# Spread products of a wide and a narrow expert block: one set for two blocks, summed in PSUM

## The reference

```python
gu = xb @ w_gate_up[e] + b_gate_up[e]                 # xb: a block of tokens of expert e
glu = jnp.minimum(gu[:, :D_FF], SWIGLU_LIMIT)
lin = jnp.clip(gu[:, D_FF:], -SWIGLU_LIMIT, SWIGLU_LIMIT)
act = glu * jax.nn.sigmoid(SWIGLU_ALPHA * glu) * (lin + 1.0)
yb = (act @ w_down[e] + b_down[e]) * g[:, None]       # g: the gate of each token
out = jnp.zeros((n_tok, d), n.dtype).at[slot_tok].add(yb.reshape(rows, d))
```

## Time and profile before

| | us |
|---|---|
| median of 3 runs | 1469.05 (1467.71 to 1469.11) |
| the profiled execution | 1468.26 |
| its span in the trace | 1466.7 |
| TensorE busy | 1449.4 (99%) |
| VectorE busy | 784.3 (53%) |
| ScalarE busy | 381.3 (26%) |
| GpSimd busy | 223.8 (15%) |

### The profile page before, as it was taken

One profiled execution on the slowest core, in us unless ns is written; L12 is line 12 of the kernel. 1 busy time (PEld: TensorE's weight loads), 2 busy tenths in 40 slices (PEclk: granted clock), 3 DMA queues, 4 the chain that ended last, 5 costly groups with the idle time before them and its releaser, 6 DMA issues.

```text
span 1466.7 us, 35402 instructions
## 1 busy us (share of the span) xinstructions
PE 1449.4 (99%) x13987; PEld 810.7 (55%) x13987; DVE 784.3 (53%) x1560; ACT 381.3 (26%) x669; POOL 223.8 (15%) x448
## 2 busy tenths in 40 slices
PE   8999999999999999999999999999999999999997
PEld 6998989977874344344443444434444344443444
DVE  6767999968646435444354443544435444354444
ACT  3634323345332012211122111221112111121114
POOL 1000000000014322121121211212112121121000
PEclk9999999999999999999999999999999999999998
DMA  3322333141339899999999999999999999999991
GB/s 135 111 69 105 116 116 114 72 177 66 116 115 346 340 383 419 401 424 419 420 424 423 424 421 415 424 423 425 418 419 425 418 423 420 417 424 418 427 417 64
DMA packets 45840, 459.46 MB, mean 313 GB/s; under 512 B 10177, under 2 KB 10690, under 8 KB 15458
## 3 DMA queue, kind: packets, MB, share of 16 engines
q1 hardware_dynamic: 37538, 450.74, 74.6%
q0 software_dynamic: 8256, 8.08, 1.7%
HBM read 456.37 MB, written 4.43 MB: 314 GB/s over the span
## 4 chain that ended last, share of the span: by engine, by line
PE 92%; DVE 4%; DMA 3%; ACT 1%; issue 0%; SPq 0%; DVEq 0%; ACTq 0%
PE bank L1937 55%; PE bank L1618 16%; PE bank L1999 10%; PE bank L1809 6%; DMA n_scratch<-reg_b 1%; DMA ring<-in_moe 1%; DVE w_lo L1035 1%; PE bank L1746 1%; PE bank L1749 1%; PE bank L1761 0%; PE bank L1747 0%; PE bank L1776 0%; DVE reg_tq L1125 0%; DVE reg_tq L1051 0%; PE bank L1637 0%
## 5 line engine op out<-in xcount | busy, mean ns | idle before, releaser
L1937 PE MATMUL bank<-ring,moe_f 128*32 128x256 f32 (+1 forms) x10296 | 835.5, 485 | 0.6 <-DVE moe_f L1530 0.4
L1937 PEld LDWEIGHTS bank<-ring,moe_f 128*32 128x32 f32 x10296 | 331.3, 110 | 500.6 <-issue 393.5
L943 ACT ACTIVATE moe_f<-moe_f 128x768 f32<-128x768 f32 (+1 forms) x32 | 23.8, 745 | 748.8 <-DVE moe_f L1517 748.8
L1552 DVE TENSOR_TENSOR reg_a<-reg_a,bank 128x512 f32<-128x512 f32 x240 | 146.7, 682 | 126.1 <-PE bank L1999 126.0
L1511 DVE STREAM_TRANSPOSE moe_f<-bank 128x768 f32<-128x768 f32 (+1 forms) x32 | 27.5, 859 | 321.6 <-PE bank L1937 315.6
L1618 PE MATMUL bank<-n_hi,w_hi 128*128 128x258 f32 (+2 forms) x608 | 190.6, 313 | 1.8 <-DVE w_lo L1035 1.8
L1618 PE MATMUL bank<-n_lo,w_hi 128*128 128x258 f32 (+2 forms) x608 | 186.4, 306 | 0.0
L1618 PE MATMUL bank<-n_hi,w_lo 128*128 128x258 f32 (+2 forms) x608 | 186.2, 306 | 0.0
L659 POOL DMA_INDIRECT moe_f<-n_scratch,idx_next x75 | 81.6, 1088 | 427.2 <-DVE moe_f L1492 410.1
L1999 PE MATMUL bank<-reg_b_r,reg_x_r 96*128 96x512 f32 (+1 forms) x504 | 144.3, 431 | 0.3 <-DVE reg_x_r L1539 0.3
L952 ACT COPY moe_f<-bank 32x256 f32<-32x256 f32 x324 | 118.0, 364 | 23.3 <-PE bank L1937 19.6
(11 more groups left out here) (301 smaller groups left out, 1181.6 us busy)
## 6 DMA issues: line engine op xcount, KB each, us to landing
ring<-in_moe SPq DMA_DIRECT2D x184, 2048.0 KB, 14.7
ring<-in_w_in SPq DMA_DIRECT2D x24, 1024.0 KB, 4.9
ring<-in_moe SPq DMA_DIRECT2D x13, 1024.0 KB, 11.7
ring<-in_w_out SPq DMA_DIRECT2D x8, 1024.0 KB, 4.8
ring<-acs_scratch SPq DMA_DIRECT2D x4, 1024.0 KB, 6.8
reg_vcs<-in_xT SPq DMA_DIRECT2D x4, 528.0 KB, 6.0
reg_x<-in_xrow SPq DMA_DIRECT2D x4, 512.0 KB, 5.2
n_scratch<-reg_b SPq DMA_DIRECT2D x4, 512.0 KB, 2.9
```

Source lines behind the costliest of these rows:

```text
L1552: v.tensor_tensor(h2[:, u // 2, c], h2[:, u // 2, c], bank[:, 5 + u % 3, :], ALU.add).then_inc(added, 1)
L1937: ins = mm(out[l * LANE:(l + 1) * LANE, g * width:(g + 1) * width], x[:, at, g * LANE:(g + 1) * LANE], w[:, l * width:(l + 1) * width], st ...
```

## The change

Blocks are added two at a time. A set now holds the wide block 2n and the narrow block 2n+1 (for n = 0 blocks 0 and 1, both wide): each unit is four products, high and low of the one and of the other, summed in the same bank, then one addition. The sets stand in the loops of the narrow blocks alone, where the eight units come in two fours with two G between them; the loops of the wide blocks, and that of block 2, have none. The wide blocks' rows are at home in `reg_b`, the narrow ones' in `reg_tq` over 64 rows; both homes get a copy of the bias rows for the first set. DVE's `add_rows` runs once for a pair, at the head of its loop body. TensorE's loops for blocks 3 and 4 are written out ahead of the loop over p.

```diff
-TURNS = "GGGGDDAAAAAAAAGGDDGGDDDD"
+TURNS = "GGGGDDGGDDGGDDDD"
+TURNS_ADDING = "GGGGDDAAAAGGAAAADDGGDDDD"
...
-        split_in, split_last = reg_b_r[:, 0:2 * D], reg_tq_r[:, 0:2 * D]
+        split_rows_of = [reg_b_r[:, 0:2 * D], reg_tq_r[:, 0:2 * D]]
+        all_w, all_n, bias_rows = slice(0, BLOCK), slice(0, NARROW * LANE), slice(BLOCK, P)
+        wide_home, narrow_home, second_home = (0, all_w), (1, all_n), (1, all_w)
...
-            def high(j, to=split_in):
-
+            def high(j, home):
+
+                n, rows = home
                 act.wait_ge(y_ready, j + 2)
-                if j is not FIRST and to is split_in:
-                    act.wait_ge(acc_done, j * UNITS)
-                a.activation(to[0:BLOCK, 0:D], y_tok[0:BLOCK, :], ACT.Copy, scale=cols[0:BLOCK, ds(j + LIST, 1)]
+                a.activation(split_rows_of[n][rows, 0:D], y_tok[rows, :], ACT.Copy, scale=cols[rows, ds(j + LIST, 1)]
                              ).then_inc(y_hi_tok, 1)
...
-            a.copy(split_in[BLOCK:P, 0:D], y_tok[BLOCK:P, :]).then_inc(gm_high, 1)
+            for n in range(2):
+                a.copy(split_rows_of[n][bias_rows, 0:D], y_tok[bias_rows, :]).then_inc(gm_high, 1)
...
             with act.Fori(0, n_pairs - 1) as p:
                 sigmoid(2 * p + 3, NARROW)
                 evict(2 * p + 2, WIDE)
-                high(2 * p + 2)
+                act.wait_ge(acc_done, p * UNITS + UNITS)
+                high(2 * p + 2, wide_home)
...
-            def add_rows(j):
+            def add_rows(n):
 
                 for u in range(UNITS):
                     c = slice(u % 2 * 512, (u % 2 + 1) * 512)
-                    dve.wait_ge(acc_done, j * UNITS + (u + 1))
+                    dve.wait_ge(acc_done, n * UNITS + (u + 1))
                     v.tensor_tensor(h2[:, u // 2, c], h2[:, u // 2, c], bank[:, 5 + u % 3, :], ALU.add).then_inc(added, 1)
...
-            dve.wait_ge(idx_moved, 1)
-            v.tensor_scalar(spread[1][0:BLOCK, :], tok_iota[0:BLOCK, :], 0.0, None, ALU.mult).then_inc(gm_low, 1)
-            dve.wait_ge(gm_high, 2)
+            dve.wait_ge(gm_high, 3)
...
-            v.tensor_tensor(split_in[BLOCK:P, D:2 * D], y_tok[BLOCK:P, :], split_in[BLOCK:P, 0:D].bitcast(F32), ALU.subtract
-                            ).then_inc(gm_low, 1)
-            split_rows(FIRST, 0, 2 * IDX_W)
-            add_rows(FIRST)
+            for n in range(2):
+                to = split_rows_of[n]
+                v.tensor_tensor(to[bias_rows, D:2 * D], y_tok[bias_rows, :], to[bias_rows, 0:D].bitcast(F32), ALU.subtract
+                                ).then_inc(gm_low, 1)
+            split_rows(FIRST, wide_home, 2 * IDX_W)
...
             with dve.Fori(0, n_pairs - 1) as p:
+                add_rows(p)
                 activations(2 * p + 3, expert_of(2 * p + 3), NARROW, (p * (16 * (WIDE + NARROW)) + 16 * (2 * WIDE + NARROW), WIDE))
-                split_rows(2 * p + 2, 0, p * (IDX_W + IDX_N) + 3 * IDX_W)
-                add_rows(2 * p + 2)
+                split_rows(2 * p + 2, wide_home, p * (IDX_W + IDX_N) + 3 * IDX_W)
                 activations(2 * p + 4, expert_of(2 * p + 4), WIDE, (p * (16 * (WIDE + NARROW)) + 32 * (WIDE + NARROW), NARROW))
-                split_rows(2 * p + 3, 1, p * (IDX_W + IDX_N) + (3 * IDX_W + IDX_N))
-                add_rows(2 * p + 3)
+                split_rows(2 * p + 3, narrow_home, p * (IDX_W + IDX_N) + (3 * IDX_W + IDX_N))
+            add_rows(n_pairs - 1)
...
+            def spread_of(home, rows, u, out, opens, closes):
+
+                to, hf = slice(u // 2 * P, (u // 2 + 1) * P), u % 2 * 512
+                split = split_rows_of[home]
+                mm(out, spread[home][rows, to], split[rows, hf:hf + 512], start=opens, stop=False)
+                return mm(out, spread[home][rows, to], split[rows, D + hf:D + hf + 512], start=False, stop=closes)
+
+            def adding_unit(n, u):
+
+                first = n is FIRST
                 if u == 0:
+                    rows_split(2 * n + 2)
+                    if not first:
+                        pe.wait_ge(added, n * UNITS)
                 if u >= 3:
+                    pe.wait_ge(added, n * UNITS + (u - 2))
+                out = bank[:, 5 + u % 3, :]
+                spread_of(0, slice(0, P) if first else all_w, u, out, True, False)
+                spread_of(1, slice(0, P) if first else all_n, u, out, False, True).then_inc(acc_done, 1)
...
-            woven(THIRD, WIDE, WIDE, 0)
+            woven(THIRD, WIDE, WIDE)
...
-            with pe.Fori(0, n_pairs - 1) as p:
-                woven(2 * p + 3, NARROW, WIDE, 1)
-                woven(2 * p + 4, WIDE, NARROW, 0)
-            woven(n_blocks - 1, NARROW, WIDE, 1)
+            pe.wait_ge(gm_high, 3)
+            pe.wait_ge(gm_low, 3)
+            woven(3, NARROW, WIDE, FIRST)
+            woven(4, WIDE, NARROW)
+            with pe.Fori(1, n_pairs - 1) as p:
+                woven(2 * p + 3, NARROW, WIDE, p)
+                woven(2 * p + 4, WIDE, NARROW)
+            woven(n_blocks - 1, NARROW, WIDE, n_pairs - 1)
```

More of the change, by code:

```diff
@@ L986, in _ @@
                 act.wait_ge(idx_moved, p * (IDX_W + IDX_N) + (3 * IDX_W + IDX_N))
-                high(2 * p + 3)
+                high(2 * p + 3, narrow_home)
             sigmoid(n_blocks - 1, NARROW)
             evict(n_blocks - 2, WIDE)
-            high(n_blocks - 2)
+            act.wait_ge(acc_done, n_pairs * UNITS)
+            high(n_blocks - 2, wide_home)
             a.activation(small[:, 7:8], ones[:, 0:1], ACT.Sqrt).then_inc(rs_root, 1)
@@ L1530, in activations, with split_rows @@
                 v.tensor_tensor(act_last if last else act_rows(n), up, sig, ALU.mult).then_inc(act_ready, 1)
-            def split_rows(j, n, columns, to=split_in):
+            def split_rows(j, home, columns):
+                n, rows = home
+                to = split_rows_of[n]
                 dve.wait_ge(idx_moved, columns)
[L1535 to L1539, removed]
+                v.tensor_scalar(spread[n][rows, :], tok_iota[rows, :], cols[rows, ds(j, 1)], None, ALU.is_equal
                                 ).then_inc(spread_ready, 1)
                 dve.wait_ge(y_hi_tok, j + 1)
[L1542 to L1545, removed]
-            def add_rows(j):
+                v.scalar_tensor_tensor(to[rows, D:2 * D], y_tok[rows, :], cols[rows, ds(j + LIST, 1)],
+                                       to[rows, 0:D].bitcast(F32), ALU.mult, ALU.subtract).then_inc(y_lo_tok, 1)
+            def add_rows(n):
                 for u in range(UNITS):
                     c = slice(u % 2 * 512, (u % 2 + 1) * 512)
-                    dve.wait_ge(acc_done, j * UNITS + (u + 1))
+                    dve.wait_ge(acc_done, n * UNITS + (u + 1))
                     v.tensor_tensor(h2[:, u // 2, c], h2[:, u // 2, c], bank[:, 5 + u % 3, :], ALU.add).then_inc(added, 1)
@@ L1561, in _ @@
             activations(SECOND, 1, WIDE, (16 * WIDE, WIDE), at=5)
-            dve.wait_ge(idx_moved, 1)
-            v.tensor_scalar(spread[1][0:BLOCK, :], tok_iota[0:BLOCK, :], 0.0, None, ALU.mult).then_inc(gm_low, 1)
-            dve.wait_ge(gm_high, 2)
-            v.tensor_tensor(spread[1][BLOCK:P, :], gm_rows[BLOCK:P, :], spread[0][BLOCK:P, :].bitcast(F32), ALU.subtract
+            dve.wait_ge(gm_high, 3)
+            v.tensor_tensor(spread[1][bias_rows, :], gm_rows[bias_rows, :], spread[0][bias_rows, :].bitcast(F32), ALU.subtract
@@ L1584, in _ @@
-            split_rows(n_blocks - 1, 1, n_pairs * (IDX_W + IDX_N) + 2 * IDX_W, split_last)
+            split_rows(n_blocks - 2, wide_home, n_pairs * (IDX_W + IDX_N) + (2 * IDX_W - IDX_N))
+            split_rows(n_blocks - 1, narrow_home, n_pairs * (IDX_W + IDX_N) + 2 * IDX_W)
             roots[0] += 1
@@ L1992, in rows_split @@
                 pe.wait_ge(y_lo_tok, n_blocks)
[L1994 to L2001, removed]
@@ L2003, in spread_unit @@
-            def spread_unit(j, u, s, out):
-                if u == 0:
[L2006 to L2011, removed]
-                if u >= 3:
-                    pe.wait_ge(added, j * UNITS + (u - 2))
-                if j is FIRST:
-                    spread_part(1, u, slice(0, P), split_in, out, True, False, (0,))
-                    return spread_part(s, u, slice(0, P), split_in, out, False)
-                return spread_part(s, u, slice(0, BLOCK), split_in, out)
@@ L2021, in woven @@
+            def woven(j, n, n_before, adds=None):
                 q = b = u = 0
-                for kind in TURNS:
+                for kind in TURNS if adds is None else TURNS_ADDING:
                     if kind == "G":
@@ L2029, in woven @@
                     else:
-                        spread_unit(FIRST if j is THIRD else j - 2, u, s, bank[:, 5 + u % 3, :]).then_inc(acc_done, 1)
+                        adding_unit(adds, u)
                         u += 1
@@ L2069, in last_bank @@
                 return bank[:, PART_BANKS[u // 2] + u % 2, :]
-            def first_part(u):
```

(5 more changed lines are left out.)

18 lines of the change are left out of this document (8 added, 10 removed).

## The result

The change makes the kernel slower: 1486.84 us (1485.62 to 1488.38, 4 runs) against 1469.08 (1467.71 to 1469.72, 4 runs), a ratio of 1.0123 with a 95% interval of 1.011 to 1.0136. The span of the profiled execution grew from 1466.7 to 1485.3 us.

The account below looks back on a forecast made before the run. Transfers were to bound the pairs at 61.0 us; 9.1 us earlier at the last wait (slack 3.4 + holes 5.7) against 3.0 for the double set gave -6.1: 1463.0 us, range 1459.2 to 1467.0.

Parts of the forecast that it names:

- Spacing of the products: In the adding sets: 0.236 us a product, so 32 products take 7.6 us; TensorE's work falls 1.5 us a pair.
- Rival (d): In the sets: something else paces them at 9.1 us, the pair stays 61.0, time within 2 us of now; chance 0.03.
- The transfers as the bound: In the pairs: DMA stays at 421 GB/s, 61.0 us a pair; TensorE waits about 1.5 us for the first down pair.
- Rival (a): In the pairs: transfers follow TensorE, the rate rising from 421 to 432 GB/s or more, time 1445; chance 0.04.
- Won back: Ahead of the third gate-up pair: three transfer holes close, 5.7 us won back, bounds 4 and 8 us.
- (e): Between 670 and 1362 us: holes add more than seen, 8 us won back and over, -9, 1459.5; chance 0.07.
- slack of 3.4: In the last narrow loop: the wide block's first down pair lands 3.4 us before use; TensorE's lead uses this up.
- The double set behind the last wait: In the last narrow loop: the whole double set takes 7.6 us instead of 4.57, unhidden, costing 3.0 us.
- VectorE, ScalarE, the prologue at nothing: Added copy, difference and moved additions, mostly around the first blocks: no cost, bound 0 to 0.5 us.
- The 2.2 us in hand for the split rows: In the narrow loop: split rows are ready at 928.5 and read at 930.76; this margin stays.

Follow-up runs that it names:

- narrow64_before: Kernel before, with the sets in the narrow blocks' loops over 64 rows, nothing alternating within a set; 1478.78 us against 1476.79 on a third chip.
- wide128: Changed kernel with the wide block's products over 128 rows and the narrow one's over 96, in all sets; 1460.93 us.
- rows96: Changed kernel with the narrow block's products over 96 rows too, rows 64 to 95 zero; 1459.61 us against 1468.24 for the kernel before, ratio 0.9942.
- one_product: rows96 with one product a unit instead of four, the wide block's rows and the narrow block's low part left out; 1457.12 us.
- rows96_early: rows96 with the first four units of a set ahead of the first two down parts; 1461.11 us against 1475.49 for the kernel before, ratio 0.9907.
- wide128_64: Changed kernel with the wide block's products over 128 rows in all sets, the narrow one's over 64; 1492.13 us against 1475.49 for the kernel before, second chip.
- rows96_again: rows96 repeated in the change's own order on the third chip; 1461.43 us against 1476.79 for the kernel before, ratio 0.9896.

## Why the prediction was wrong, point by point

- **Spacing of the products, the step that failed.** "A product over 64 rows costs no less, since its 512 columns stay; I take the same 0.236", with bounds of 0.227 and 0.285. By itself that holds (narrow64_before, 4.55 us a set). What I left out is the order in which 96 and 64 rows stand: 0.33 us on average, a set of 10.6 us instead of 7.6, above my upper bound of 9.1. With that TensorE's own work rises by 1.5 us a pair instead of falling by 1.5. I had bounded the cost by the sets of the trace, and in all of those the row count is the same throughout.
- **The row that was there.** The timeline of the kernel before has four products in its tail that alternate just so (start, us):

```profile
1456.19 0.73 PE L1999 MATMUL bank<-reg_b_r,reg_x_r 96*128 96x512 f32 x2
1456.85 0.73 PE L1999 MATMUL bank<-reg_tq_r,reg_x_r 64*128 64x512 f32 x2
```

  1456.85 - 1456.19 = 0.66 us for two, the number of the changed kernel. The row of fourteen products of 64 rows, shown with narrow64_before, stands just in front of it at 0.23 us a product. 15 sets with the 0.66: 7.7 us for the first (128 rows) and 14 x 10.6 = 148.4, together 156.1, against the 138.1 of before: +18.0 us. Measured are +17.8 in the median and +18.6 in the span. The Trainium skill, "TensorEngine Tiling (Array Packing)", section "Key Properties", says it outright: changing the tiling mode drains TensorE, and its "Tiling Modes" list 64 rows as a mode of their own. It gives no price; the runs give 0.2 us, and the weight loads of the changed kernel, which don't run ahead behind a change, agree with it. It doesn't say what 96 rows count as; wide128 does. Rival (d) had this shape, but with a set of 9.1 us, and so ended in "same".
- **The transfers as the bound.** The mechanism was right, though it didn't come into play in the changed kernel, where TensorE is slower than they are. With the row counts equal (rows96) the pair is 60.55 us, the waits stand where they were forecast and the time is 8.6 us lower instead of 6.1. The bound itself was a little too long: 421 GB/s was the rate at TensorE's pace of 61.0 us, and with TensorE waiting it is 424. So TensorE waits about 0.8 us a pair in rows96 and not 1.5. Rival (a), 432 GB/s or more, is out by one_product.
- **Won back.** I took 5.7 us of holes. The first two are closed in rows96: its windows 539 to 546 and 606 to 609 us carry 427 and 431 GB/s, where the kernel before had 231 and 229. The last set of rows96 (start, us):

```profile
1407.11 0.50 PE L1997 MATMUL bank<-reg_b_r,reg_x_r 96*128 96x512 f32 x1
```

  The two gate-up transfers on either side of the down pair that was waited for are issued at 1387.5 and 1394.4 in this run and land 11.9 and 14.9 us later, at 1399.4 and 1409.3. In the kernel before it was 1407.7 and 1417.8, so they land about 8.4 us earlier, not 5.7: this is the term that was mis-sized for rows96, and it lies in the range of (e). With the slack of 3.4 that gives 11.8, and the set starts 11.6 us earlier than the 1418.76 of the earlier trace rows. The 2.7 us beyond the holes come from the loop, where a pair is 60.55 instead of 61.00, which I had called next to none; how they divide between a higher rate and small gaps wasn't measured.
- **The double set behind the last wait, 3.0 us.** The sum for rows96, -11.6 + 3.0 = -8.6, meets the measured 8.6. As the 11.6 is itself measured, this bears out the 3.0 alone.
- **VectorE, ScalarE, the prologue at nothing.** Held: in the expert part of the changed kernel no wait for any of them is longer than 0.5 us. The 2.2 us in hand for the split rows is borne out by rows96_early: with the set 2.6 us (DD) further forward, a wait of 0.5 us came up.

## What to carry to other kernels

Before products of different shapes are put in turn, look at the row counts: with 96 and 128 rows in turn they follow each other every 0.23 us at 512 columns, and each change between 64 rows and more costs 0.2 us, about one such product. Fill up with zero rows rather than change, or group by shape. And bound a new sequence by a row that has its alternation, not only its parts: such a row is often in the trace, in a corner that the change doesn't touch.

## What the runs showed of the hardware

- A change between 64 and 96 or 128 rows in TensorE's products: 0.20 to 0.21 us each; between 96 and 128 none that shows (0.23 us a product).
- Behind a change the weight load starts with its product (869.67 us both in the changed kernel), without one 0.23 us ahead of it.
- Twelve products 0.43 us apart were followed by a granted clock of 0.50, and in that kernel it came back in pair after pair: 71.7 us instead of 61.0. With products 0.33 us apart it stayed at 1.00. So 0.1 us a product more than in the changed kernel, 3.2 us a pair by itself, made 9 us a pair. That the spacing is the cause wasn't tested by itself.
- A wait can be followed by the lower clock too: behind the one wait of 2.4 us in rows96 the granted clock was 0.57 from 678 to 682 us, and the two D took 4.48 us instead of 2.80; behind its waits of 0.3 to 1.1 us they took 2.80.
- The sixteen DMA engines moved 423 or 424 GB/s over 600 us and longer in six runs whose TensorE has less work than the transfers (rows96 and its repeat, its three other orders, one_product), and never more; windows of 2 to 4 us show up to 446.
- Between three chips the kernel before differed by 1 to 9 us (1468.24, 1475.49 and 1476.79). On the second and the third the longer piece of expert products takes 48.6 us (wide128_64, rows96_again) instead of 48.30.
